# Expert weights in transfers of 4 MB with rows of 32 KB, and a feed-forward on rows that are scaled afterwards

## The chip, the cores and the metric

One Trainium2 chip (trn2), one of its cores. The metric is the device time of the whole program in microseconds (us); the kernel before ran three times, with a median of 1717.28 us (1716.75 to 1719.55).

## What is computed

Two transformer blocks, one behind the other, batch 1, width D = 1024, all in f32. The first has 272 rows (16 meta tokens and 256 of input): a norm, differential attention beside a gated convolution, and a feed-forward of 16 experts, each of which takes its 34 best rows:

```python
logits = hs @ w_router; aff = softmax(logits); g, idx = top_k(aff.T, 34)
xg = hs[idx]
y = einsum('ecf,efd->ecd', silu(xg @ w_gate) * (xg @ w_up), w_down) * g[..., None]
out = zeros((L, D)).at[idx.reshape(-1)].add(y.reshape(-1, D))
```

w_gate and w_up are 1024 x 2048 for each expert, w_down 2048 x 1024: 8 MB each, 24 MB for an expert, 384 MB (402.7 million bytes) for all. The second block works on 256 rows. Of it only the end matters here:

```python
x = x + merged @ w_out[l]
h2 = rms_norm_2(x, norm2_g[l])          # x * rsqrt(mean(x*x) + 1e-6) * g
x = x + jnp.square(jax.nn.relu(h2 @ w_ff1[l])) @ w_ff2[l]
```

w_ff1 is 1024 x 4096, w_ff2 4096 x 1024. Since relu(s a)^2 = s^2 relu(a)^2 for a positive s, the scale of a row can be left out of h2 and the row of the result multiplied by 1 / (mean(x*x) + 1e-6).

## The kernel before

The five engines each run a list of instructions written out by hand (`pe_program`, `act_program`, `dve_program`, `pool_program`, `sp_program`). They meet at named events: `mark("pe_moe", "used", slot)` counts a semaphore up, `at("used", slot)` is the value to wait for. TensorE's results stand in eight PSUM banks of 128 x 512 f32; `room(bank, ...)` waits until what the bank held before has been taken out.

**Expert weights.** A ring of 20 slots in SBUF, each of 128 partitions x 2048 f32 (1 MB, 8 KB in a partition), holds the weights. An expert has 24 slots: 16 for gate and up (k = 0 to 7, two matrices), 8 for down. They are numbered from 16 on (`expert_slot`, L430), so expert 0 has 16 to 39 and expert 15 has 376 to 399; `ring_slot` (L425) gives the place. SyncE fetches two slots with one DMA (`fetch_pair`, L2718), 2 MB in rows of 16 KB, except at two places (`HALVED`, L51) where it fetches single slots. Before it issues, it waits until TensorE has used the slots that stood there, 20 slots earlier (`freed`, L2685). All its DMAs run in one queue: the first block's weights, the experts', then those of the second block, 160 raw pieces of 512 KB (`fetch_raw`, L2742), into three buffers that lie where ring slots were. `brought(i)` (L435) names the fetch with which slot i came; TensorE waits for it in `gate_up` (L674) and `down` (L717).

**Order in an expert.** TensorE multiplies gate and up (L690), two column groups side by side, then for even experts scatters the pair of experts before (L707), turns the hidden rows (L714) and multiplies down (L728). ScalarE makes the SiLU (L1319) and copies Y (L1333, L1334), VectorE multiplies (L2010). In the first expert TensorE also gathers the rows between the k-steps (L670). In the last expert ScalarE rounds the first three raw pieces of the second block (`hi`, L1307) before it copies Y.

**Second block.** Every weight piece of 128 x 1024 is split into a rounded part (`hi`, ScalarE, L1307) and a remainder (`lo`, VectorE, L1991), in four buffers; products are made from three passes over parts. `quad` (L1113) multiplies one piece into four banks, 4 + 2 ti + db (ti: half of the rows, db: half of the columns), for the output projection (`h2o`) and for the second product of the feed-forward (`ff2`).

**Between h2o and the feed-forward.** VectorE adds the four banks into H (L2471). ScalarE squares each (L1654), VectorE makes the mean (L2477), POOL the power -1/2 (L2662), VectorE and ScalarE scale one half of the rows each into `XB2` (L2480, L1657). TensorE turns them (`turn_two`, L753), VectorE multiplies by the gain (L2036), ScalarE rounds (L1345), VectorE and POOL make the remainders (L2041, L2565). TensorE waits for all of these (`normed`, L756) before the first of 32 tiles of the feed-forward (`tile_sides`, L780; matmuls L787, L788, L790). The bank of each tile, and of each turned group in `turn_two`, is drawn from one cycle of six banks, `rot` (L744), that runs through the whole second block. Behind each tile ScalarE copies half of it (L1673), VectorE adds (L2494) and squares (L2496), ScalarE rounds (L1662), VectorE makes the remainder (L2488), in eight buffers `RL`. After `ff2` VectorE adds the four banks into H (L2506) and ScalarE stores them (L1682).

Of the kernel before, what the change touches and what calls it, by code (L numbers as in the profile page):

```python
# [191 lines left out]
class Memory:  # L192


    def __init__(self, nc):
# [55 lines left out]
        self.ring_pair = [sb(f"ring{s}", ring0 + 4096 * s, 4096) for s in range(RING // 2)]  # L251
        self.ring = [self.ring_pair[s // 2][:, 2048 * (s % 2):2048 * (s % 2) + 2048] for s in range(RING)]
# [143 lines left out]
        self.XB2 = late[:, 0:2048].rearrange("p (t c) -> p t c", t=2)  # L396
        self.tmp2 = [late[:, 2048:3072], late[:, 6144:7168]]
# [56 lines left out]
def pe_program(pe, m, sig, banks):  # L454
# [677 lines left out]
    turn_two(m.XB2, "h2")  # L1132
    normed("h2")
# [9 lines left out]
def act_program(act, m, sig, banks, t):  # L1143
# [520 lines left out]
    for i in range(32):  # L1664
# [14 lines left out]
    for ti in range(2):  # L1679
        for db in range(2):  # L1680
# [29 lines left out]
def dve_program(dve, m, sig, banks, t):  # L1710
# [755 lines left out]
    for ti in range(2):  # L2466
        for db in range(2):
# [4 lines left out]
    for ti in range(2):  # L2472
        x, y = m.fr[:, 8 + 2 * ti:9 + 2 * ti], m.fr[:, 9 + 2 * ti:10 + 2 * ti]
        dve.wait_ge(*at("s2", ti, 1))
        e.tensor_scalar(x, x, y, None, ALU.add).then_inc(*mark("dve_norm2", "s2 sum", ti))
        dve.wait_ge(*now("dve_norm2"))
        e.tensor_scalar(x, x, 1.0 / D, EPS, ALU.mult, ALU.add).then_inc(*mark("dve_norm2", "mean h2", ti))  # L2477
        dve.wait_ge(*at("power h2", ti))
        if ti == 0:
            e.tensor_scalar(m.XB2[:, 0, :], H[:, 0, :], x, None, ALU.mult).then_inc(*mark("dve_norm2", "h2", 0))  # L2480
        else:
            e.tensor_copy(m.fr[:, 10:11], x).then_inc(*mark("dve_norm2", "h2 scale", 1))
    turned("h2", m.vec[:, V_N2:V_N2 + 8], m.tmp2)
# [6 lines left out]
    for i in range(32):  # L2490
# [11 lines left out]
    for ti in range(2):  # L2502
        for db in range(2):
# [407 lines left out]
```

## Time and profile before

| | us |
|---|---|
| median of three runs | 1717.28 |
| the profiled execution | 1717.86 |
| its span | 1716.1 |
| TensorE matmuls busy | 1481.4 (86%) |
| VectorE busy | 564.4 (33%) |
| ScalarE busy | 413.9 (24%) |
| POOL busy | 107.6 (6%) |
| DMA, 511.5 MB, mean | 298 GB/s |

The span runs from the first to the last instruction of the profiled execution; its own time is 1.8 us longer. All times in the rows count from the start of the span. A busy TensorE is not TensorE at its peak: matmuls overlap, and half of the clock doubles them. A row of a stretch gives busy time and count for each engine, the granted clock of TensorE (1.00 is 2.4 GHz, 0.50 is 1.2 GHz), the share in which the 16 DMA engines were busy, and the rate.

### The profile page before, as it was taken

Reading aid. Unit: us, or ns where it says so; the run is one execution under the profiler, and the core shown is the slowest. Engines: PE = TensorE matmul, PEld = TensorE weight load, DVE = VectorE, ACT = ScalarE, POOL = GpSimd, SP = SyncE. Lnnn points to the kernel's source line nnn. Section 1 sums busy time; section 2 is a strip of 40 time slices with the busy share of each in tenths; the row PEclk is TensorE's granted clock in tenths of the full one; section 3 lists DMA queues with packets and bytes.
Section 4 is the critical chain, followed back from the end, with each engine's and each line's share of the span. In section 5 each row is a group of like instructions: output and inputs, shape, how many; then the busy total and the mean of one; then the engine's idle time right before and its main releaser. Section 6 shows DMA issues by size and latency. Waiting matters only on the chain.

```text
span 1716.1 us, 18717 instructions
## 1 busy us (share of the span) xinstructions
PE 1481.4 (86%) x7789; PEld 880.6 (51%) x7789; DVE 564.4 (33%) x966; ACT 413.9 (24%) x850; POOL 107.6 (6%) x117
## 2 busy tenths in 40 slices
PE   7999799977877878778778778699998999989999
PEld 7684433322222222222222222287897899968887
DVE  6573300100101001001001010385874555858843
ACT  5342010000000000000000000246642564445532
POOL 2010000000000000000000000021420210500000
PEclk9999799999999999999999999989999999989999
DMA  9235799999999999999999999744331334535564
GB/s 383 114 105 239 293 427 427 427 427 427 427 427 427 426 427 427 427 427 427 427 426 427 427 427 427 291 135 131 134 111 36 126 116 152 181 123 185 184 201 142
DMA packets 55989, 511.50 MB, mean 298 GB/s; under 512 B 6481, under 2 KB 6737, under 8 KB 28897
## 3 DMA queue, kind: packets, MB, share of 16 engines
q1 hardware_dynamic: 54144, 506.11, 73.3%
q10 hardware_dynamic: 1760, 4.19, 0.7%
q8 instruction: 62, 1.02, 0.2%
q14 instruction: 23, 0.18, 0.0%
HBM read 509.23 MB, written 1.05 MB: 297 GB/s over the span
## 4 chain that ended last, share of the span: by engine, by line
PE 56%; DMA 35%; DVE 4%; ACT 3%; issue 1%; POOL 0%; ACTq 0%; DVEq 0%; SPq 0%; POOLq 0%
DMA sb_ring<-in_w_gate_up 33%; PE PS L771 10%; PE PS L690 7%; PE PS L728 7%; PE PS L1118 6%; PE PS L807 4%; PE PS L788 4%; DMA sb_raw<-in_w 2%; PE PS L880 2%; PE PS L600 2%; PE PS L707 2%; PE PS L787 2%; PE PS L490 1%; PE PS L493 1%; PE PS L498 1%
## 5 line engine op out<-in xcount | busy, mean ns | idle before, releaser
L690 PE MATMUL PS<-sb_ring,sb_XG 128*64 128x512 f32 x2048 | 466.4, 601 | 120.3 <-DMA sb_ring<-in_w_gate_up 120.0
L690 PEld LDWEIGHTS PS<-sb_ring,sb_XG 128*64 128x64 f32 x2048 | 142.7, 137 | 438.4 <-issue 228.8
L2010 DVE TENSOR_TENSOR sb_SL<-sb_SL,PS 128x512 f32<-128x512 f32 x32 | 20.5, 683 | 792.4 <-PE PS L690 792.4
L728 PE MATMUL PS<-sb_ring,sb_HT 128*64 128x512 f32 x1024 | 226.1, 595 | 28.6 <-DMA sb_ring<-in_w_down 14.1
L1991 DVE TENSOR_TENSOR sb_wp<-sb_raw,sb_wp 128x1024 fp32r<-128x1024 f32 x160 | 206.7, 1294 | 115.2 <-ACT sb_wp L1307 113.9
L1307 ACT CAST sb_wp<-sb_raw 128x1024 fp32r<-128x1024 f32 x160 | 166.9, 1045 | 124.4 <-PE PS L1118 56.3
L771 PE MATMUL PS<-sb_hr,sb_wp 128*128 128x256 f32 x1440 | 183.7, 289 | 6.2 <-DVE sb_hr L2041 3.5
L771 PEld LDWEIGHTS PS<-sb_hr,sb_wp 128*128 128x128 f32 x1440 | 178.5, 196 | 10.0 <-issue 6.5
L728 PEld LDWEIGHTS PS<-sb_ring,sb_HT 128*64 128x64 f32 x1024 | 82.0, 137 | 162.4 <-issue 116.3
L1319 ACT ACTIVATE sb_SL<-PS 128x512 f32<-128x512 f32 x32 | 17.4, 595 | 516.8 <-PE PS L690 516.8
L788 PE MATMUL PS<-sb_hr,sb_wp 128*128 128x512 f32 x256 | 90.0, 405 | 3.4 <-DVE sb_hr L2041 3.4
L807 PE MATMUL PS<-sb_wp,sb_hr 128*128 128x512 f32 x336 | 83.8, 404 | 4.4 <-ACT sb_SUV L1384 4.2
L1118 PE MATMUL PS<-sb_wp,sb_fh 128*128 128x512 f32 x384 | 87.2, 389 | 0.0
L1118 PEld LDWEIGHTS PS<-sb_wp,sb_fh 128*128 128x128 f32 x384 | 72.1, 188 | 14.9
L807 PEld LDWEIGHTS PS<-sb_wp,sb_hr 128*128 128x128 f32 x336 | 63.4, 193 | 18.7 <-issue 6.1
L1333 ACT COPY sb_Y<-PS 64x512 f32<-64x512 f32 x16 | 9.2, 578 | 237.8 <-PE PS L728 237.8
L787 PE MATMUL PS<-sb_hr,sb_wp 128*128 128x256 f32 x224 | 63.4, 283 | 0.0
L2554 POOL TENSOR_TENSOR sb_sm<-sb_sm 128x1 f32<-128x1 f32 x2 | 1.1, 548 | 945.7 <-DVE sb_sm L2051 945.7
L788 PEld LDWEIGHTS PS<-sb_hr,sb_wp 128*128 128x128 f32 x256 | 47.0, 193 | 12.7 <-issue 3.7
L787 PEld LDWEIGHTS PS<-sb_hr,sb_wp 128*128 128x128 f32 x224 | 43.3, 193 | 1.6
L707 PE MATMUL PS<-sb_Y,sb_GT 128*128 128x512 f32 x64 | 31.3, 634 | 4.0 <-ACT sb_Y L1334 4.0
L2654 POOL TENSOR_TENSOR sb_NN<-sb_NN,sb_SC 128x256 f32<-128x256 f32 x24 | 25.4, 1059 | 96.2 <-DVE sb_SC L2454 93.4
(396 smaller groups left out, 1357.8 us busy)
## 6 DMA issues: line engine op xcount, KB each, us to landing
sb_ring<-in_w_gate_up SPq DMA_DIRECT2D x127, 2048.0 KB, 45.2
sb_ring<-in_w_down SPq DMA_DIRECT2D x63, 2048.0 KB, 45.2
sb_raw<-in_w SPq DMA_DIRECT2D x160, 512.0 KB, 4.0
sb_ring<-in_w_in SPq DMA_DIRECT2D x12, 1024.0 KB, 15.9
sb_ring<-in_w_out SPq DMA_DIRECT2D x4, 1024.0 KB, 13.9
sb_ring<-in_w_gate_up SPq DMA_DIRECT2D x2, 1024.0 KB, 9.7
sb_ring<-in_w_down SPq DMA_DIRECT2D x2, 1024.0 KB, 45.0
sb_KW<-in_kw SPq DMA_DIRECT2D x1, 1403.0 KB, 34.7
```

Source lines behind the costliest of these rows:

```text
L600: ins = e.matmul(PS[0:n, b, :], m.mixT[:, c, c0:c0 + n], w[:, o:o + 512], start=(c == 0), stop=(c == 7))
L690: ins = e.matmul(PS[64 * g:64 * g + 64, b, :], m.XG[:, k, r0:r0 + 64], m.ring[s][:, (2 * g + q) * 512:(2 * g + q) * 512 + 512], start=(k = ...
L707: e.matmul(PS[:, b, :], m.GT[:, ti, :], m.Y[:, db * 512:db * 512 + 512], start=True, stop=True).then_inc(*mark("pe_moe", "in", "sc", p, ti ...
L728: ins = e.matmul(PS[64 * g:64 * g + 64, b, :], m.HT[:, c % 8, (c // 8) * 64:(c // 8) * 64 + 64], m.ring[s][:, a * 1024 + g * 512:a * 1024 ...
L771: ins = e.matmul(PS[:, b, 0:256], lhs(p1, k), rhs(p2, k), start=(k == 0 and q == 0), stop=(k == K - 1 and q == 2))
L787: e.matmul(PS[:, b, 0:256], lo[:, k, :], m.hT[0][:, k, :], start=False, stop=False)
L788: ins = e.matmul(PS[:, b, :], hi[:, k, :], m.hT2[:, k, :, :], start=(k == 0), stop=(k == 7))
L807: ins = e.matmul(PS[:, b, :], m.hT[p1][:, k, ti * 128:ti * 128 + 128], w[p2][:, k2 * 512:k2 * 512 + 512], start=(k == 0 and q == 0), stop= ...
L880: ins = e.matmul(PS[:, b, r * 128:r * 128 + 128], lhs(4 * q + r), rhs(4 * q + r), start=True, stop=True)
L1118: ins = e.matmul(PS[:, b, :], acts[p1][:, k, ti * 128:ti * 128 + 128], w[p2][:, db * 512:db * 512 + 512], start=(k == 0 and q == 0), stop= ...
L1307: e.copy(m.wp_hi[n % WR], m.raw[raw_turn(n) % RAW]).then_inc(*mark("act_split", "hi", n))
L1991: e.tensor_tensor(m.wp_lo[n % WR], m.raw[raw_turn(n) % RAW], m.wp_hi[n % WR].bitcast(F32), ALU.subtract).then_inc(*mark("dve_split", "lo", n))
```

## The change

Three things are changed for the experts' weights. The array in HBM is laid out so that four slots lie in one row of 32 KB. SyncE fetches slots 44 to 395 four at a time, 4 MB in one DMA, and waits until all four places are free; slots 16 to 43 and 396 to 399 are fetched as before. TensorE waits for the fetch that brought its slot.

In the second block the scale of h2 is left out. TensorE turns H itself, for 256 columns of both row halves into one bank, and needs for that only the column half whose adds are done; `quad` and the adds go through the column halves first. ScalarE makes the rounded part from PSUM with the gain as scale, 128 x 256 for each k, VectorE the remainder in the same way. TensorE waits for them k by k. The sums of squares are made by ScalarE behind tiles 4 and 6, mean and reciprocal by VectorE behind tiles 8 and 10, and the last adds multiply by it. POOL has no part in this norm any more, and `XB2` and its temporaries are gone.

```diff
+PAIRS = tuple(range(16, 24 + RING, 4)) + (16 + 24 * 16 - 4,)
...
-        self.ring_pair = [sb(f"ring{s}", ring0 + 4096 * s, 4096) for s in range(RING // 2)]
-        self.ring = [self.ring_pair[s // 2][:, 2048 * (s % 2):2048 * (s % 2) + 2048] for s in range(RING)]
+        self.ring_four = [sb(f"ring{s}", ring0 + 8192 * s, 8192) for s in range(RING // 4)]
+        self.ring = [self.ring_four[s // 4][:, 2048 * (s % 4):2048 * (s % 4) + 2048] for s in range(RING)]
...
 def brought(i):
+    if i - i % 4 not in PAIRS:
+        return i - i % 4
     return i if i - i % 2 in HALVED else i - i % 2
...
     def tile_sides(n, *tile):
         hi, lo = (x.rearrange("p (k c) -> p k c", k=8) for x in piece(n))
         b = room(next(rot), *tile)
         for k in range(8):
+            pe.wait_ge(*at("h2 hi", k))
+            pe.wait_ge(*(at("out", "h2", k // 2) if k % 2 else at("h2 lo", k)))
...
     def quad(k, last, acts, w, name):
-        for ti in range(2):
-            for db in range(2):
+        for db in range(2):
+            for ti in range(2):
...
-    turn_two(m.XB2, "h2")
-    normed("h2")
+    for j in range(4):
+        b = room(j, "h2", j)
+        for k2 in range(2):
+            for ti in range(2):
+                pe.wait_ge(*at("out", "h2o", ti, j // 2))
+                c = 256 * j + 128 * k2
+                ins = e.transpose(PS[:, b, 256 * k2 + 128 * ti:256 * k2 + 128 * ti + 128], m.H[:, ti, c:c + 128], ident)
+        ins.then_inc(*mark("pe_norm", "in", "h2", j))
...
-    act.wait_ge(*at("in", "h2o", 1, 1))
-    for ti in range(2):
-        for db in range(2):
-            act.wait_ge(*at("out", "h2o", ti, db))
-            e.activation(m.RL[:, 2 * ti + db, :, :].rearrange("p q c -> p (q c)"), H[:, ti, db * 512:db * 512 + 512], ACT.Square,
-                         accum_out=m.fr[:, 8 + 2 * ti + db:9 + 2 * ti + db]).then_inc(*mark("act_norm2", "s2", ti, db))
-    act.wait_ge(*at("h2 scale", 1))
-    e.activation(m.XB2[:, 1, :], H[:, 1, :], ACT.Copy, scale=m.fr[:, 10:11]).then_inc(*mark("act_norm2", "h2", 1))
-    turned("h2", m.tmp2)
+    for k in range(8):
+        act.wait_ge(*at("in", "h2", k // 2))
+        act.wait_ge(*at("in", "h2o", 1, 1))
+        e.mul(m.hT[0][:, k, :], PS[:, banks.of("h2", k // 2), 256 * (k % 2):256 * (k % 2) + 256],
+              m.vec[:, V_N2 + k:V_N2 + k + 1]).then_inc(*mark("act_norm2", "h2 hi", k))
+
+    def row_sums(ti):
+        act.wait_ge(*now("act_sums"))
+        e.activation(m.JKf, H[:, ti, :], ACT.Square, accum_out=m.fr[:, 8 + ti:9 + ti]).then_inc(*mark("act_sums", "sums", "h2", ti))
...
+        if i in (4, 6):
+            row_sums(i // 2 - 2)
...
+    for k in range(8):
+        j = k // 2
+        event = ("out", "h2", j) if k % 2 else ("h2 lo", k)
+        dve.wait_ge(*at("h2 hi", 2 * j + 1))
+        e.scalar_tensor_tensor(m.hT[1][:, k, :], PS[:, banks.of("h2", j), 256 * (k % 2):256 * (k % 2) + 256], m.vec[:, V_N2 + k:V_N2 + k + 1],
+                               m.hT[0][:, k, :].bitcast(F32), ALU.mult, ALU.subtract).then_inc(*mark("dve_norm2", *event))
...
+        if i in (8, 10):
+            r = m.fr[:, 4 + i // 2:5 + i // 2]
+            dve.wait_ge(*at("sums", "h2", i // 2 - 4))
+            e.tensor_scalar(r, r, 1.0 / D, EPS, ALU.mult, ALU.add).then_inc(*mark("dve_norm2", "mean h2", i // 2 - 4))
+            dve.wait_ge(*now("dve_norm2"))
+            e.reciprocal(r, r).then_inc(*mark("dve_norm2", "h2 scale", i // 2 - 4))
...
-            e.tensor_tensor(hv, hv, PS[:, banks.of("ff2", ti, db), :], ALU.add).then_inc(*mark("dve_ff", "out", "ff2", ti, db))
+            dve.wait_ge(*at("h2 scale", ti))
+            e.scalar_tensor_tensor(hv, PS[:, banks.of("ff2", ti, db), :], m.fr[:, 8 + ti:9 + ti], hv, ALU.mult, ALU.add).then_inc(*mark("dve_ff", "out", "ff2", ti, db))
...
-    def fetch_pair(i, src):
+    def fetch_four(i, src):
+        for j in range(4):
+            if brought(i + j) == i + j:
+                n = sum(brought(i + q) == i + j for q in range(4))
+                s, o = ring_slot(i + j), 2048 * j
+                for q in range(n):
+                    for event in freed(i + j + q):
+                        sp.wait_ge(*at(*event))
+                e.dma_start(m.ring_four[s // 4][:, o:o + 2048 * n], src[:, o:o + 2048 * n]).then_inc(*mark(f"ring{s}", "w", i + j, by=16))
```

## Rows read from the trace of the kernel before

**Rows 1.** The page: the span, and the DMA rates of 40 slices.
```profile
span 1716.1 us, 18717 instructions
...
GB/s 383 114 105 239 293 427 427 427 427 427 427 427 427 426 427 427 427 427 427 427 426 427 427 427 427 291 135 131 134 111 36 126 116 152 181 123 185 184 201 142
```

**Rows 2.** The chain in order of time (start us, length us, what), end of the experts.
```profile
1063.17 35.68 DMA sb_raw<-in_w
1098.87 1.05 ACT sb_wp L1307
```

**Rows 3.** Stretches: busy time of each engine, TensorE's clock, DMA share, GB/s.
```profile
34.00:44.00 10.00, 10.00 (x77) 9.77 (x76) 6.12 (x9) 5.11 (x8) 3.30 (x3) 1.00 1.01 419
...
616.00:675.00 59.00, 44.99 (x196) 14.56 (x196) 5.30 (x10) 2.83 (x5) 0.00 (x0) 1.00 1.01 427
```

**Rows 4.** The page: DMA issues, count, KB each, median us from issue to landing.
```profile
sb_ring<-in_w_gate_up SPq DMA_DIRECT2D x127, 2048.0 KB, 45.2
```

**Rows 5.** Pair fetches (L2727): issued 126-200, at 193.0, 202-213, at 217.0; later issues.
```profile
DMA to landing us min/median/max: 7.7/10.9/18.5
...
DMA to landing us min/median/max: 9.0/9.0/9.0
...
L2727 SPq DMA_DIRECT2D sb_ring<-in_w_gate_up x3: 328/328/328, 202.6 to 212.2; - x3
...
DMA to landing us min/median/max: 10.1/10.2/10.3
...
DMA to landing us min/median/max: 10.4/10.4/10.4
...
225.17 0.33 SPq L2727 DMA_DIRECT2D sb_ring<-in_w_gate_up  x1
L2727 SPq DMA_DIRECT2D sb_ring<-in_w_down x3: 328/328/328, 242.9 to 249.8; - x3
```

**Rows 6.** Timeline of the last expert: start, length, engine, line, operation, idle before.
```profile
1075.55 3.65 PE L690 MATMUL PS<-sb_ring,sb_XG 128*64 128x512 f32 x16 [2.00 <-DMA sb_ring<-in_w_gate_up]
1082.30 7.09 PE L728 MATMUL PS<-sb_ring,sb_HT 128*64 128x512 f32 x32 [0.98 <-DVE sb_HT L2024]
1090.12 7.09 PE L728 MATMUL PS<-sb_ring,sb_HT 128*64 128x512 f32 x32 [0.73 <-DMA sb_ring<-in_w_down]
```

**Rows 7.** Timeline from the output projection to the feed-forward, and its second product.
```profile
1518.63 2.65 PE L1118 MATMUL PS<-sb_wp,sb_hr 128*128 128x512 f32 x11
1520.88 2.47 DVE L2471 TENSOR_TENSOR sb_H<-sb_H,PS 128x512 f32<-128x512 f32 x4
1532.88 0.77 PE L788 MATMUL PS<-sb_hr,sb_wp 128*128 128x512 f32 x1 [3.38 <-DVE sb_hr L2041]
...
1538.37 0.37 ACT L1673 COPY sb_late<-PS 128x256 f32<-128x256 f32 x1 [6.55 <-PE PS L788]
...
1625.10 7.21 PE L1118 MATMUL PS<-sb_wp,sb_fh 128*128 128x512 f32 x31
```

**Rows 8.** TensorE's clock around that norm and at the kernel's start.
```profile
1525.00:1526.00 1.00, 0.85 (x4) 0.85 (x5) 0.37 (x3) 0.00 (x0) 0.52 (x1) 0.50 0.00 0
...
8.64 4.51 PE L474 MATMUL PS<-sb_cst,sb_XN 128*128 128x128 f32 x24 [8.64 <-DVE sb_sm L1722]
...
16.00:18.00 2.00, 2.00 (x11) 2.00 (x12) 2.00 (x6) 2.00 (x3) 0.00 (x0) 0.58 1.01 418
18.00:20.00 2.00, 2.00 (x11) 2.00 (x11) 2.00 (x4) 0.40 (x1) 0.00 (x0) 0.57 1.02 422
```

**Rows 9.** Groups by line (count, busy us, mean ns), and the feed-forward's stretch.
```profile
L2461 DVE SCALAR_TENSOR_TENSOR sb_hr<-sb_NN,sb_hr 128x256 fp32r<-128x256 f32 x8 | 3.7, 531 | 0.0
L2454 DVE SCALAR_TENSOR_TENSOR sb_SC<-sb_R,PS 128x256 f32<-128x256 f32 x14 | 5.6, 412 | 2.0 <-POOL sb_NN L2654 2.0
L1645 ACT ACTIVATE sb_hr<-sb_NN 128x256 fp32r<-128x256 f32 x8 | 2.6, 403 | 1.8 <-PE PS L771 1.8
...
1535.00:1625.00 90.00, 90.00 (x507) 78.34 (x506) 73.96 (x123) 50.12 (x92) 0.00 (x0) 0.98 0.55 180
```

More of the change, by code:

```diff
@@ L1678, in act_program @@
         hi(P_FF2 + i + 3)
-    for ti in range(2):
-        for db in range(2):
+    for db in range(2):
+        for ti in range(2):
             act.wait_ge(*at("out", "ff2", ti, db))
@@ L2463, in dve_program @@
         lo(P_OUT + c + 3)
-    for ti in range(2):
-        for db in range(2):
+    for db in range(2):
+        for ti in range(2):
             hv = H[:, ti, db * 512:db * 512 + 512]
@@ L2471, in dve_program @@
             e.tensor_tensor(hv, hv, PS[:, banks.of("h2o", ti, db), :], ALU.add).then_inc(*mark("dve_merge", "out", "h2o", ti, db))
[L2472 to L2483, printed above, removed]
+    for k in range(8):
[4 more added lines that the diff above has]
+                               m.hT[0][:, k, :].bitcast(F32), ALU.mult, ALU.subtract).then_inc(*mark("dve_norm2", *event))
     def hidden_lo(i):
@@ L2501, in dve_program @@
         lo(P_FF2 + i + 3)
-    for ti in range(2):
-        for db in range(2):
+    for db in range(2):
+        for ti in range(2):
             hv = H[:, ti, db * 512:db * 512 + 512]
             dve.wait_ge(*at("in", "ff2", ti, db))
-            e.tensor_tensor(hv, hv, PS[:, banks.of("ff2", ti, db), :], ALU.add).then_inc(*mark("dve_ff", "out", "ff2", ti, db))
+            dve.wait_ge(*at("h2 scale", ti))
+            e.scalar_tensor_tensor(hv, PS[:, banks.of("ff2", ti, db), :], m.fr[:, 8 + ti:9 + ti], hv, ALU.mult, ALU.add).then_inc(*mark("dve_ff", "out", "ff2", ti, db))
 def pool_program(pool, m, sig, banks, t):
@@ L2655, in pool_program @@
             n += 1
-    for ti in range(2):
-        x = m.fr[:, 8 + 2 * ti:9 + 2 * ti]
-        pool.wait_ge(*at("mean h2", ti))
-        pool.wait_ge(*now("pool_norm"))
-        e.tensor_tensor(x, x, mhalf[:, 0:1], ALU.pow).then_inc(*mark("pool_norm", "power h2", ti))
-    first_half_lo("h2", m.tmp2)
 def sp_program(sp, m, sig, banks, t):
@@ L2716, in fetch @@
         e.dma_start(m.ring[s], src).then_inc(*mark(f"ring{s}", "w", i, by=16))
-    def fetch_pair(i, src):
-        if i in HALVED:
-            fetch(i, src[:, 0:2048])
-            fetch(i + 1, src[:, 2048:4096])
-        else:
-            s = ring_slot(i)
-            for event in freed(i) + freed(i + 1):
-                sp.wait_ge(*at(*event))
-            e.dma_start(m.ring_pair[s // 2], src).then_inc(*mark(f"ring{s}", "w", i, by=16))
+    def fetch_four(i, src):
[7 more added lines that the diff above has]
+                e.dma_start(m.ring_four[s // 4][:, o:o + 2048 * n], src[:, o:o + 2048 * n]).then_inc(*mark(f"ring{s}", "w", i + j, by=16))
     for i in range(12):
@@ L2733, in sp_program @@
     for ex in range(NE):
-        for k in range(8):
-            fetch_pair(expert_slot(ex, 2 * k), t["w_gate_up"][ex, k])
-        for s in range(4):
-            fetch_pair(expert_slot(ex, 16 + 2 * s), t["w_down"][ex, s])
+        for k in range(4):
+            fetch_four(expert_slot(ex, 4 * k), t["w_gate_up"][ex, k])
+        for s in range(2):
+            fetch_four(expert_slot(ex, 16 + 4 * s), t["w_down"][ex, s])
     done = {}
@@ L2845, in layout @@
     a["w_out"] = pack_R(i["w_out"][0])
-    a["w_gate_up"] = np.concatenate([i[n][0].reshape(NE, 8, 128, 2048) for n in ("w_gate", "w_up")], 3)
-    a["w_down"] = np.ascontiguousarray(i["w_down"][0].reshape(NE, 4, 4, 128, D).transpose(0, 1, 3, 2, 4)).reshape(NE, 4, 128, 4 * D)
+    g = np.stack([i[n][0].reshape(NE, 4, 2, 128, 2048) for n in ("w_gate", "w_up")], 3)
+    a["w_gate_up"] = np.ascontiguousarray(g.transpose(0, 1, 4, 2, 3, 5)).reshape(NE, 4, 128, 8192)
+    a["w_down"] = np.ascontiguousarray(i["w_down"][0].reshape(NE, 2, 8, 128, D).transpose(0, 1, 3, 2, 4)).reshape(NE, 2, 128, 8 * D)
     v = np.zeros((P, NVEC), np.float32)
```

9 lines of the change are left out of this document (2 added, 7 removed).

## The prediction, made before the changed kernel was run

> **What bounds the kernel now.** I read the page first, then the chain of waits, stretches of the timeline and the DMA queue of SyncE. The page [rows 1] gives 1716.1 us of span and a strip of DMA rates in which twenty of forty slices stand at 426 or 427 GB/s: in the middle something is limited by transfers. The chain in order of time [rows 2] shows how that stretch ends: behind the expert weights stand the first raw weights of the second block (35.68 us from issue to landing), then ScalarE's rounding of them, then its copy of the last expert's output. So between about 200 us and 1100 us the DMA stream sets the time, and what shortens it moves all that comes after. From 1100 us on TensorE is the bound, with one hole that this change touches, the norm between the second block's output projection and its feed-forward.
>
> The stream's own pace: with rows of 16 KB it moves 427 GB/s, with rows of 8 KB (the first block's weights) 419 GB/s [rows 3], each with a DMA share of 1. Per engine, a sixteenth, a 16 KB row takes 16384 B / 26.69 = 613.9 ns and an 8 KB row 8192 B / 26.19 = 312.8 ns. Two short rows take 11.7 ns more than one long row: a cost per row. The neighbouring windows read 420 GB/s in places, which makes 10.3 ns of it; I take 10.9.
>
> **Part 1: longer rows.** Before, the experts come in transfers of 2 MB, 127 of them for gate and up alone [rows 4]. Slots 16 to 43 and 396 to 399 stay as they were; the 352 slots between them go from 176 pairs to 88 fours. Each engine then moves 8 rows of 32 KB where it moved 16 of 16 KB: 88 x 8 = 704 rows fewer on each engine. At 10.9 ns that is **-7.7 us** (-7.3 to -8.2). No transfer in this trace has rows above 16 KB, so the outer ends are 0 (the cost goes with bytes above some length) and a loss (a rival below). I take the straight line because 8 and 16 KB lie next to 32.
>
> The trace's row costs 10.9 ns. The Trainium skill ("DMA: Bandwidth & Descriptors", the section on why small descriptors are slow) states a fixed overhead of about 3 cycles per packet; with the 850 MHz of the same page that is an estimate of 3.5 ns, so 704 rows would bring 2.5 us and not 7.7. Measured rows say more than the page, and I go by them; the page's value is a rival below.
>
> **Part 2: what a coarser grain costs where the ring is nearly dry.** SyncE may issue a transfer only when TensorE has used all its slots. In the first expert it is just in time: a pair is issued every 4.8 us while one takes 4.9 us to move. Three issues from 202.6 to 212.2 us show that, the second of them (slots 42 and 43) landing at 207.4 + 10.2 = 217.6 us. The issue at 217.0 us (slots 46 and 47, after slot 27 is used) lands 10.4 us later, at 227.4 us; the one at 193.0 us, into an empty queue, needs 9.0 us, and the quickest 2 MB up to 200 us needs 7.7 us [rows 5]. Since 4.9 us of these are movement, the start of a transfer takes 2.8 to 4.1 us. Slots 44 to 47, so far two issues (212 and 217 us), become one, at 217.0. It finds a queue that is about to end, at 217.6 us, and lands at 217.0 + 2.8 to 4.1 + 9.7 = 229.5 to 230.8 us instead of 227.4: 2.1 to 3.4 us of the stream are lost and never come back. I take **+2.8**. The next fours are issued when slots 31, 35 and 39 are used. The pairs that waited for the first and the last of these were issued at 225.2 and 242.9 us [rows 5], slot 35 is used 7.1 us before slot 39 [rows 6], at 235.8, against queue ends near 230, 240 and 249.5: leads of 4 us and more, so no second hole, and the lead grows from there. In the median 45.2 us pass from issue to landing [rows 4], so later about four fours are always queued, and TensorE's 7.1 us for a four instead of 3.65 for a pair [rows 6] take nothing from the stream. In SyncE's queue only the raw weights stand behind the experts', and they are asked for 35 us before they land [rows 2].
>
> **Part 3: the end of the experts.** The last two k-steps of gate and up (slots 388 to 391) now arrive together, when the last pair of them did, so TensorE ends gate and up 3.4 us later against the stream. Before, it took up the last pair at 1075.55 for 3.65 us, began the down projection at 1082.30 (3.1 us of SiLU and turning between), had caught up with the stream at 1090.12 and finished at 1097.2; ScalarE was busy with the raw weights until 1099.92 and only then copied [rows 6]. Laid out again with fours: 7.1 us of gate and up from 1075.5, the same 3.1 us, and 14.1 us for the eight slots of down, which are then all there, end at 1099.8. That is 0.1 us before ScalarE: the cover is all but gone. The four is 9.7 us on its way and 7.1 in work; TensorE's pauses of some 2.6 us between could cost it the clock once; half speed for the 3.4 us that such a fall lasts in [rows 8] is 1.7 us. I charge **+0.3** (0 to +1.7).
>
> **Part 4: the feed-forward on unscaled rows.** Before, TensorE ends the output projection at 1521.3; the adds into H run to 1523.35; then squares, POOL's power, scaling, 16 transposes, gains, rounding and remainders, and the first matmul of the feed-forward starts at 1532.88, 11.6 us after the last [rows 7]. The change takes POOL, the squares, the scaling and four 128x512 temporaries out of this path. New path, from rows: VectorE begins its adds at 1520.9 (it makes the remainder of the third piece first), so the first two adds end at 1522.2, the four at 1523.4. Four transposes per bank, 0.19 us each at the kernel's start [rows 8], put bank 0 there at about 1523.1. ScalarE: eight products of 128x256 at 0.40 us (the nearest rounding row) from 1523.1, two before VectorE begins at 1523.95. VectorE: eight remainders at 531 ns (the same operation and output type; 412 ns is that of one that reads PSUM and writes plain f32) end at 1523.95 + 4.25 = 1528.2 [rows 9]. The first tile of the feed-forward looks as if it could follow k by k, but its bank is the one of the fourth h2 bank (the turning list of six banks stands at 3 there, since the norm no longer draws four from it), which is released by the last remainder. So it starts at 1528.3: **-4.6 us** (-5.6 with 412 ns).
>
> The granted clock is the second term. From 1525 us on it is at half [rows 8], 3.7 us into TensorE's idleness, and the first tile takes 5.5 us (1532.88 to 1538.37) instead of the 2.8 us of the others (31 tiles to 1625.1 [rows 7]): 2.7 us. After the change TensorE rests 0.9 us, transposes for 3 us, rests 3.1 us. The nearest case in the trace is the kernel's start: 24 transposes from 8.64 to 13.15 at a full clock, a rest of 2.75 us, and a mean clock of 0.58 and 0.57 in the 4 us from 16, which makes 3.4 us at half [rows 8]. So I take one such fall behind the rest: 1.7 of the 2.7 us still lost, **-1.0 us** (0 to -2.7). The Trainium skill ("TensorE: Matmul & The Clock Gate", PE-mode transpose) says that transposes do not count as busy for the gate; by it the rest would be 7 us in one and all 2.7 us would stay lost. The rows at the kernel's start speak against it, weakly.
>
> What moves elsewhere: the row sums go to ScalarE beside tiles 4 and 6 (two of about 1.25 us, where it is busy 50 of 90 us), their mean and reciprocal to VectorE beside tiles 8 and 10 (four of about 0.2 us, where it is busy 74 of 90 us [rows 9]). A tile leaves VectorE 0.3 us spare and there are eight buffers and four pieces of lead, so I cost them at nothing; without that cover it would be 0.8 us. The four last adds become fused ones: 412 against 421 ns in the two forms at 128x256, so 0. The new order of quadrants keeps the matmuls and 0.
>
> **Sum.** -7.7 + 2.8 + 0.3 - 4.6 - 1.0 = -10.2 us. The profiled execution took 1717.86 us for a span of 1716.1, and becomes 1707.7; the median of three before is 1717.28, 0.6 lower, so 1707.1. With all bounds one way it is -14 (1703), the other way -6.4 (1711).
>
> **Rivals.** *Length buys nothing*: the engines cut or pace rows so that 32 KB cost twice 16 KB. For it: no row of that length is here. Then -2.5, 1714.8 us. *The page's 3.5 ns*: -5.0, 1712.3 us. *The feed-forward gives nothing net*: the start comes earlier, but the clock stays low longer or VectorE, late with pieces, holds the next tiles; against it, VectorE's spare time. Then -4.6, 1712.7 us. *Slower, by the pace of long rows*: the sixteen engines read places twice as far apart, and the stream falls to the slowest saturated pace that a row shows, 419 GB/s. The 88 fours are 369.1 MB: 880.9 us instead of 864.4, +16.5 in place of -7.7, so 1731.3 us. It decides from a pace of 425.8 GB/s down, where the loss eats the 2.5 us of the rest; that the pace rises from 8 to 16 KB speaks against it.
>
> **How the numbers follow.** Forecast 0.66; nothing from length 0.10; the page's value 0.10; no feed-forward gain 0.09; slower pace 0.05. 0.2% (3.4 us) is about what a measurement of this kernel can tell from no change. The forecast, the page's value and the third rival lie below 1713.9: 0.85 faster. The first rival is the 0.09 within the bound; the slower pace, and a little of the first, is 0.06. The range goes from 1702.5 to 1714.0, over the forecast's own 1703 to 1711 to the two rivals at 1712.
>
> **What would show it.** Right: 431 GB/s in the middle; an expert each 58.3 us instead of 58.9; a hole of 2 to 3 us in the stream near 218 us; ScalarE's copy of the last Y about 5 us earlier; no more than 7.5 us between the last matmul of the output projection and the first of the feed-forward. Wrong: 427 GB/s or less, holes in the stream at later experts, the last Y copy waiting for TensorE, or a first tile of 5.5 us.

## The result, and the profile after

The kernel after takes **1704.78 us** (median of four runs, 1703.32 to 1705.47); the kernel before, run beside it, 1718.41. The ratio is 0.992, with a 95% interval of 0.9903 to 0.9937: faster, by 0.6% to 1.0%. The profiled execution took 1705.39 us, 12.5 us less than the one of before, and its span is shorter by the same 12.5 us. The page, first the span and the rates, then the DMA issues:

```profile
span 1703.6 us, 18612 instructions
...
GB/s 383 117 100 222 305 406 430 430 432 433 430 430 430 429 430 433 430 430 430 430 430 433 431 433 430 321 123 144 121 103 58 122 112 151 176 157 186 185 196 138
...
sb_ring<-in_w_gate_up SPq DMA_DIRECT2D x59, 4096.0 KB, 39.9
sb_ring<-in_w_down SPq DMA_DIRECT2D x29, 4096.0 KB, 41.3
```

Beside [rows 1]: slices of 427 have become 429 to 433, and one, the sixth, has fallen from 427 to 406. That one (213 to 256 us) holds the hole in the stream. The 88 fours are there (59 and 29), and about four of them are under way at a time (39.9 us at 9.7 each). The packets that the page counts in SyncE's queue fall from 54144 to 41472. The difference is 16 times 792, so 792 on each of the 16 engines: the 704 rows of the prediction and 88 more, one for each transfer that is saved. A row of 32 KB is not cut in two.

The same stretches as [rows 3] and around 217 us, kernel after:

```profile
330.00:1050.00 720.00, 587.29 (x2522) 199.79 (x2518) 43.61 (x78) 35.14 (x62) 0.00 (x0) 0.96 1.00 431
214.50:216.00 1.50, 1.50 (x10) 0.44 (x7) 0.00 (x0) 0.00 (x0) 0.00 (x0) 1.00 0.79 339
216.00:217.50 1.50, 1.50 (x10) 0.69 (x7) 0.00 (x0) 0.00 (x0) 0.00 (x0) 1.00 0.03 11
217.50:219.00 1.50, 1.50 (x10) 0.85 (x10) 0.44 (x1) 1.22 (x2) 0.00 (x0) 1.00 1.31 350
```

And kernel before:

```profile
330.00:1050.00 720.00, 571.52 (x2518) 188.36 (x2514) 43.61 (x78) 35.12 (x62) 0.00 (x0) 1.00 1.01 427
...
216.00:217.50 1.50, 1.50 (x11) 0.71 (x6) 0.00 (x0) 0.00 (x0) 0.00 (x0) 1.00 0.89 382
```

The last column is the rate: 431 against 427 GB/s in the long stretch, 11 against 382 in the 1.5 us of the hole. The column before last but one, TensorE's clock, says something that the prediction did not have: 0.96 instead of 1.00 over 720 us, so about 58 us of them at half clock. Its busy time grows by 16 us for the same work and costs nothing, as TensorE waits for weights there anyway.

The fetch of slots 44 to 47, kernel after (issue, and time to landing), which stands against the last two landings of [rows 5]:

```profile
L2730 SPq DMA_DIRECT2D sb_ring<-in_w_gate_up x1: 328/328/328, 217.1 to 217.1; - x1
...
DMA to landing us min/median/max: 13.5/13.5/13.5
```

The end of the experts and the scatter, kernel after, timeline of TensorE and ScalarE:

```profile
1060.19 7.09 PE L692 MATMUL PS<-sb_ring,sb_XG 128*64 128x512 f32 x32 [2.64 <-DMA sb_ring<-in_w_gate_up]
1069.90 8.64 PE L692 MATMUL PS<-sb_ring,sb_XG 128*64 128x512 f32 x32 [2.63 <-DMA sb_ring<-in_w_gate_up]
...
1081.65 13.95 PE L730 MATMUL PS<-sb_ring,sb_HT 128*64 128x512 f32 x64 [0.99 <-DVE sb_HT L2033]
...
1094.85 1.05 ACT L1318 CAST sb_wp<-sb_raw 128x1024 fp32r<-128x1024 f32 x1 [0.22 <-DMA sb_raw<-in_w]
1095.92 0.58 ACT L1344 COPY sb_Y<-PS 64x512 f32<-64x512 f32 x1
...
1097.15 3.70 PE L709 MATMUL PS<-sb_Y,sb_GT 128*128 128x512 f32 x8 [1.55 <-ACT sb_Y L1345]
```

The scatter of the kernel before:

```profile
1101.18 5.40 PE L707 MATMUL PS<-sb_Y,sb_GT 128*128 128x512 f32 x8 [3.97 <-ACT sb_Y L1334]
```

ScalarE's third rounding begins at 1094.85 instead of 1098.87 [rows 2]: the experts end 4.0 us earlier. TensorE is done at 1081.65 + 13.95 = 1095.60, ScalarE at 1095.90: the cover, 2.7 us before, has shrunk to 0.3 us. The scatter takes 1.7 us less, as the clock does not fall in it.

From the output projection to the feed-forward, kernel after:

```profile
1515.47 2.47 DVE L2480 TENSOR_TENSOR sb_H<-sb_H,PS 128x512 f32<-128x512 f32 x4
1516.20 0.14 PEld L1143 LDWEIGHTS PS<-sb_cst,sb_H 128*128 128x128 f32 x1 [0.76 <-DVE sb_H L2480]
...
1516.80 2.18 PE L1143 MATMUL PS<-sb_cst,sb_H 128*128 128x128 f32 x15 [0.27 <-DVE sb_H L2480]
1517.39 3.03 ACT L1664 ACTIVATE sb_hr<-PS,sb_vec 128x256 fp32r<-128x256 f32 x8 [3.09 <-PE PS L1143]
...
1518.26 3.23 DVE L2485 SCALAR_TENSOR_TENSOR sb_hr<-PS,sb_vec,sb_hr 128x256 fp32r<-128x256 f32 x8 [0.32 <-ACT sb_hr L1664]
...
1521.75 0.47 PE L793 MATMUL PS<-sb_hr,sb_wp 128*128 128x512 f32 x1 [2.76 <-DVE sb_hr L2485]
...
1524.80 0.37 ACT L1680 COPY sb_late<-PS 128x256 f32<-128x256 f32 x1 [3.45 <-PE PS L793]
...
1612.46 0.70 PE L1123 MATMUL PS<-sb_wp,sb_fh 128*128 128x512 f32 x2 [1.01 <-DVE sb_late L2497]
```

The last matmul of the output projection ends at 1515.87, so 5.9 us lie between it and the first tile, where 11.6 were. The first tile waits until the last of eight remainders (L2485) has run, and takes 3.05 us (1521.75 to 1524.80) where it took 5.49 [rows 7]. The last line is new: TensorE waits 1.0 us before `ff2`, for VectorE's add behind the last tile (L2497).

| from before to after, profiled executions | before | after | difference |
|---|---|---|---|
| start of the last scatter | 1101.18 | 1097.15 | -4.0 |
| scatter until the projections of the second block | 20.11 | 18.44 | -1.7 |
| projections until the end of the output projection | 399.99 | 400.28 | +0.3 |
| from there to the first tile | 11.60 | 5.88 | -5.7 |
| first tile until `ff2` | 92.22 | 90.71 | -1.5 |
| `ff2` until the end | 91.0 | 91.1 | +0.1 |
| span | 1716.1 | 1703.6 | -12.5 |

### The profile page after: what moved, and what is told of

It reads as the page before. It is cut to its first block, busy times and chain, and to the rows that moved or that the text cites. A ratio compares the mean times of both kernels' runs of the same rounds, so it can differ in the third digit from the quotient of the medians.

```text
span 1703.6 us, 18612 instructions
## 1 busy us (share of the span) xinstructions
PE 1490.3 (87%) x7789; PEld 888.2 (52%) x7789; DVE 560.7 (33%) x966; ACT 413.2 (24%) x849; POOL 103.6 (6%) x113
## 4 chain that ended last, share of the span: by engine, by line
PE 57%; DMA 34%; DVE 4%; ACT 3%; issue 1%; POOL 0%; ACTq 0%; SPq 0%; DVEq 0%; POOLq 0%
DMA sb_ring<-in_w_gate_up 29%; PE PS L773 10%; PE PS L692 9%; PE PS L730 6%; PE PS L1123 6%; PE PS L812 4%; PE PS L793 4%; DMA sb_raw<-in_w 3%; DMA sb_ring<-in_w_down 2%; PE PS L885 2%; PE PS L602 2%; PE PS L792 2%; PE PS L709 2%; PE PS L492 1%; PE PS L500 1%
## 5 line engine op out<-in xcount | busy, mean ns | idle before, releaser
L692 PE MATMUL PS<-sb_ring,sb_XG 128*64 128x512 f32 x2048 | 479.6, 623 | 110.1 <-DMA sb_ring<-in_w_gate_up 110.1
L692 PEld LDWEIGHTS PS<-sb_ring,sb_XG 128*64 128x64 f32 x2048 | 152.0, 143 | 431.8 <-issue 274.8
L812 PE MATMUL PS<-sb_wp,sb_hr 128*128 128x512 f32 x336 | 84.0, 404 | 4.4 <-ACT sb_SUV L1395 4.3
L812 PEld LDWEIGHTS PS<-sb_wp,sb_hr 128*128 128x128 f32 x336 | 63.4, 193 | 18.6 <-issue 6.1
L793 PEld LDWEIGHTS PS<-sb_hr,sb_wp 128*128 128x128 f32 x256 | 45.8, 188 | 11.6 <-ACT sb_wp L1318 3.0
L492 PE MATMUL PS<-sb_hnhi,sb_wh 128*128 128x272 f32 x160 | 27.8, 320 | 4.7 <-ACT sb_hnhi L1189 3.3
## 6 DMA issues: line engine op xcount, KB each, us to landing
sb_ring<-in_w_gate_up SPq DMA_DIRECT2D x59, 4096.0 KB, 39.9
sb_ring<-in_w_down SPq DMA_DIRECT2D x5, 2048.0 KB, 13.6
```

Source lines behind the costliest of these rows:

```text
L492: e.matmul(PS[:, b, 0:L], hi[:, k, :], m.hnp[0][:, k, :], start=(k == 0), stop=False)
L692: ins = e.matmul(PS[64 * g:64 * g + 64, b, :], m.XG[:, k, r0:r0 + 64], m.ring[s][:, (2 * g + q) * 512:(2 * g + q) * 512 + 512], start=(k = ...
L812: ins = e.matmul(PS[:, b, :], m.hT[p1][:, k, ti * 128:ti * 128 + 128], w[p2][:, k2 * 512:k2 * 512 + 512], start=(k == 0 and q == 0), stop= ...
```

## The experiments

Ten kernels. The kernel before took 1717.22 us beside `experts_only`, `feedforward_only`, `pairs_to_56` and `banks_shifted`, 1717.07 beside `rows16_in_4mb`, `grain_alone`, `all_mended` and `rows32_in_2mb`, and 1717.72 beside `rows16_half_partitions` and `rows32_every_second`. Beside the kernel after it took 1718.41, 1.2 to 1.3 us more than beside the first eight, so part of a difference between medians of different series is this shift; each ratio goes by its own series. My theory was the sum of the prediction; the rivals were that the number or size of the transfers brings the gain and not the length of the rows, that the feed-forward gives nothing net, and, for what is still lost, that the hole, the last four and the wait on bank 3 are not its causes.

**One half at a time.** `experts_only` has the diff's hunks on `PAIRS`, `ring_four`, `brought`, `fetch_four` and the layout in HBM, `feedforward_only` all the others.

> The expert part of the change alone, the feed-forward as before. My theory by the traces of before and after: ScalarE's third rounding of raw weights, which ended at 1099.92 us before, ends 4.0 us earlier, and the scatter behind it runs at the full clock (3.7 us instead of 5.4), so the sum is -5.7 us against the kernel before, the stretch from 1121 us on as long as before. The rival, that nearly all of the gain is the feed-forward's and the 4 MB transfers only change the noise, wants -1 us or less here.

> The feed-forward part alone, transfers as before. My theory: the first matmul of the feed-forward 5.7 us earlier against the end of the output projection, 2.4 us because its first tile runs at the full clock, and 1.0 us lost at the start of the second product, where bank 4 is held by the last tile: together -7.1 us against the kernel before. If the clock falls in the shorter rest all the same, -5. If the two parts add up, this and the experts alone come to the -12.5 us of the whole change's span.

The experts alone: 1709.51 us (1708.38 to 1710.63), ratio 0.9955 (0.9942 to 0.9969), -7.7 us. The feed-forward alone: 1712.14 (1710.12 to 1713.06), 0.9972 (0.9961 to 0.9984), -5.1 us. Both halves are faster by themselves, and -7.7 and -5.1 together are -12.8, where the whole has -12.5 in the profiled executions and -13.6 in the medians: neither lives on the other. Each is some 2 us from what I expected, in opposite directions. The traces say where most of it lies. The start of the last scatter moves by -3.6 us with the experts alone (-4.0 in the kernel after), and the rest before the first tile by -5.7 us with the feed-forward alone, as in the kernel after. But a long stretch of block 2 that no edit touches, from the first product behind its twelve tiles of queries, keys and values (L807 before, L812 after) to the start of its output projection, took 339.8 us in the one and 343.7 in the other, against 341.4 before. So a sum of parts is good to about 2 us and no better.

**Length, number or grain.** Two kernels keep the waits of the kernel after, but the layout in HBM is that of before, with rows of 16 KB.

`rows16_in_4mb` has 88 transfers of 4 MB, and each row of the ring is filled from two rows of 16 KB:

```diff
-                e.dma_start(m.ring_four[s // 4][:, o:o + 2048 * n], src[:, o:o + 2048 * n]).then_inc(*mark(f"ring{s}", "w", i + j, by=16))
+                if n == 4:
+                    e.dma_start(m.ring_four[s // 4].rearrange("p (k c) -> p k c", k=2), src.rearrange("k p c -> p k c")).then_inc(*mark(f"ring{s}", "w", i + j, by=16))
...
```

`grain_alone` has 176 pairs of 2 MB, but SyncE waits for four free slots and then issues two pairs, and TensorE waits for both:

```diff
+    def arrived(slot):
+        pe.wait_ge(*at("w", brought(slot)))
+        if slot - slot % 4 not in PAIRS:
+            pe.wait_ge(*at("w", brought(slot) + 2))
...
+                for q in range(0, n, 2) if n == 4 else (0,):
...
```

> The changed kernel, with 4 MB in one transfer as before the run, but HBM laid out as in the kernel before, so that a transfer moves rows of 16 KB, two for each partition. If the cost hangs on the row (my theory), the stream between 330 and 1050 us stands at 427 GB/s and the third rounding of raw weights ends about 7 us later than in the changed kernel (1095.9 us), near 1103 us. If it hangs on the number of transfers, 431 GB/s and 1096 us.

> The changed kernel with transfers of 2 MB in rows of 16 KB as before the change, but both waits in fours: SyncE issues two pairs when four places are free, TensorE starts when four slots are there. It has the cost of the grain without the gain of the rows. My theory: a hole of about 3 us in the stream at 216 us, 427 GB/s after it, TensorE's clock falling in the pauses as in the changed kernel (about 20 falls against 1 before), the third rounding at 1103 us, 3 us after that of the kernel before. If long transfers and not the grain make the hole, there is none and 1100 us.

`rows16_in_4mb`: 1713.45 us (1711.74 to 1714.21, ten runs), ratio 0.9977 (0.9968 to 0.9987). `grain_alone`: 1715.13 (1712.87 to 1718.74, ten runs), 0.999 (0.9981 to 1.0). The interval of the second reaches 1.0, so it can't be told from the kernel before. The long stretch of both, `rows16_in_4mb` first, and for `grain_alone` the 3 us of the hole too:

```profile
330.00:1050.00 720.00, 582.72 (x2505) 197.32 (x2502) 43.61 (x78) 35.15 (x62) 0.00 (x0) 0.96 1.01 427
```

```profile
330.00:1050.00 720.00, 582.21 (x2512) 221.31 (x2510) 43.69 (x78) 35.14 (x62) 0.00 (x0) 0.96 1.01 427
216.00:219.00 3.00, 3.00 (x18) 1.50 (x16) 0.44 (x1) 1.39 (x2) 0.00 (x0) 1.00 0.46 98
```

Both stay at 427 GB/s, the pace of before: it is the rows of 32 KB that bring the 431, and not the transfers of 4 MB. The kernel after differs from `rows16_in_4mb` by the rows alone, and its median is 8.7 us lower. Of that, the traces give the rows 6.5 us: ScalarE's third rounding ends at 1095.90 against 1102.40. The profiled executions are 6.3 us apart, since a fall of the clock in the first tile of `rows16_in_4mb` (1.6 us more) and a shorter way from the projections to the output projection (1.7 us less) nearly cancel. Against the kernel before, with its third rounding at 1099.92, `rows16_in_4mb` is 2.5 us late and `grain_alone` (1103.14) 3.2: that is the hole, and the 0.7 us between them may be the 88 packets that the first saves on each engine. Of the 5.1 us that the feed-forward gives alone, 3.6 are left in `rows16_in_4mb` and 1.9 in `grain_alone`. In `grain_alone` the Y copy waits 2.6 us for TensorE (it ends at 1105.73, ScalarE at 1103.14), as the last four comes late there. And a clock of 0.95 or 0.96 in the long stretch comes with all kernels of this grain that keep the stream, whatever their rows.

**The hole alone.** Slots 16 to 55 in pairs instead of 16 to 43.

```diff
-PAIRS = tuple(range(16, 24 + RING, 4)) + (16 + 24 * 16 - 4,)
+PAIRS = tuple(range(16, 56, 4)) + (16 + 24 * 16 - 4,)
```

> The changed kernel with pairs up to slot 55 and fours from slot 56 on. My theory: the hole in the DMA stream at 216 us goes (3.2 us), three fours less save 0.26 us less, so the third rounding of raw weights ends 3 us earlier, -3 us against the changed kernel. Rival: the stream makes the hole good later, since TensorE has spare time in the experts, and the end stays where it is.

1706.68 us (1703.02 to 1707.48), ratio 0.9933 (0.992 to 0.9945): not faster than the kernel after, so my -3 us was wrong. The hole is gone, and ScalarE's third rounding ends at 1093.20 instead of 1095.90. Then two things take the gain. Stretch, TensorE and ScalarE of this kernel:

```profile
216.00:219.00 3.00, 3.00 (x18) 1.68 (x18) 0.44 (x1) 1.67 (x2) 0.00 (x0) 1.00 0.97 415
```

```profile
1078.65 15.65 PE L730 MATMUL PS<-sb_ring,sb_HT 128*64 128x512 f32 x64 [0.99 <-DMA sb_ring<-in_w_down]
```

```profile
1094.34 0.58 ACT L1344 COPY sb_Y<-PS 64x512 f32<-64x512 f32 x1 [1.14 <-PE PS L730]
```

The down projection takes 15.65 us instead of 13.95, one fall of the clock, and ends at 1094.30, 1.1 us after ScalarE. So TensorE, which the prediction had ready 0.1 us ahead of ScalarE, is now the later one: of 2.7 us, 1.6 reach the scatter. The rest went in the stretch that no edit touches. First the kernel after, then this one:

```profile
1152.53:1493.86 341.33, 323.97 (x2226) 289.65 (x2225) 213.14 (x353) 172.67 (x416) 75.12 (x72) 0.98 0.37 123
```

```profile
1151.18:1495.89 344.71, 328.02 (x2227) 292.74 (x2225) 212.92 (x353) 172.68 (x416) 75.12 (x72) 0.97 0.36 122
```

The same matmuls take 3.4 us longer at a lower mean clock (0.97 against 0.98), with VectorE and ScalarE busy for the same time. Over the ten traces that keep the stream, the stretch goes from 339.8 us (a clock of 0.99, `experts_only` and `grain_alone`) to these 344.7 (0.97), so the time follows the clock; why a run gets more or fewer falls is open.

**The bank.** The prediction said that the first tile could follow the norm k by k but for its bank. Two draws from the cycle of banks ahead of the tiles give it another:

```diff
+    next(rot), next(rot)
     for i in range(32):
         tile_sides(P_FF1 + i, "ff1", i).then_inc(*mark("pe_ff", "in", "ff1", i))
```

> The changed kernel with two more draws from the cycle of six banks, so that the first tile of the feed-forward has a bank that is free at once and the last tile is not in bank 4. My theory: the 1.0 us pause before the second product goes, and the first tile follows the remainders k by k instead of waiting for the last of them, so that it ends about 2.3 us earlier: -3 us against the changed kernel, 1701.5 us. If the pause of VectorE's remainders is what counts and not the bank, -1 us or nothing.

1700.82 us (1699.58 to 1704.3), ratio 0.9909 (0.9895 to 0.9922). The median is 4.0 us below that of the kernel after, 2.8 us if each is set against its own runs of the kernel before, and the intervals of the two ratios overlap; the trace decides:

```profile
1514.80 2.18 PE L1143 MATMUL PS<-sb_cst,sb_H 128*128 128x128 f32 x15 [0.27 <-DVE sb_H L2481]
1516.89 0.47 PE L793 MATMUL PS<-sb_hr,sb_wp 128*128 128x512 f32 x1
...
1606.76 0.62 PE L1123 MATMUL PS<-sb_wp,sb_fh 128*128 128x512 f32 x2
```

```profile
1516.26 3.23 DVE L2486 SCALAR_TENSOR_TENSOR sb_hr<-PS,sb_vec,sb_hr 128x256 fp32r<-128x256 f32 x8 [0.32 <-ACT sb_hr L1665]
```

The first tile starts at 1516.89, while VectorE still makes remainders, 3.0 us after the output projection instead of 5.9. `ff2` starts with no idle time in its row, so the new 1.0 us pause was the same cycle of banks: with six banks and 32 tiles, the four draws that the norm no longer makes had moved the last tile from bank 2 to bank 4, which `ff2` needs first, and two more draws move it to bank 0. From the output projection to `ff2` the two make 96.6 - 92.9 = 3.7 us.

**All together.** Pairs up to slot 55, pairs for slots 388 to 395, and the shifted banks.

> The changed kernel with pairs up to slot 55, the fours from 388 and 392 as pairs again, and the six banks shifted by two. My theory: ScalarE's third rounding at 1093.3 us (no hole) and TensorE done with the last expert before it, so that the scatter starts 1.3 us after that; the first tile of the feed-forward starts 3 us after the output projection instead of 5.9 and the second product without a pause: -2.5 and -4 us, 1698 us, give or take the 2 us by which the stretch between 1155 and 1490 us differs from run to run. Rival: TensorE rests longer before the scatter and its clock falls there as before the change: 1.7 us of it come back.

**1699.44 us** (1697.46 to 1702.57), ratio 0.9896 (0.9881 to 0.9911), the lowest of all: its median is 5.3 us below that of the kernel after, 4.0 us if each is set against its own runs of the kernel before. Stretch, TensorE and ScalarE:

```profile
216.00:219.00 3.00, 3.00 (x18) 1.54 (x16) 0.44 (x1) 1.08 (x2) 0.00 (x0) 1.00 0.99 426
```

```profile
1084.77 7.07 PE L730 MATMUL PS<-sb_ring,sb_HT 128*64 128x512 f32 x32
1095.06 3.70 PE L709 MATMUL PS<-sb_Y,sb_GT 128*128 128x512 f32 x8 [3.23 <-ACT sb_Y L1346]
```

No hole (426 GB/s), and with pairs at the end TensorE is done at 1091.84, 2.0 us ahead of ScalarE: the scatter starts at 1095.06, 2.1 us before that of the kernel after. It takes 3.70 us behind a rest of 3.23, so the rival's fall of the clock did not come. Its interval overlaps that of `banks_shifted` (1.4 us apart), so only the trace shows what the pairs add. A last comparison of this kind, pairs at the end alone, was not run.

**Half of the partitions.** I wanted long rows in small transfers, and cut each four into its partitions 0 to 63 and 64 to 127:

```diff
+                if n == 4:
+                    for h in range(2):
+                        r = slice(64 * h, 64 * h + 64)
+                        event = ("w", i + j) if h else ("w half", i + j)
+                        e.dma_start(m.ring_four[s // 4][r, :], src[r, :]).then_inc(*mark(f"ring{s}", *event, by=16))
...
```

> The changed kernel, with rows of 32 KB but each four as two transfers of 2 MB over 64 partitions each. If the cost hangs on the row: 431 GB/s and the third rounding ends at 1096 us, as in the changed kernel. If on the number of transfers: 427 GB/s and 1103 us.

2613.89 us (2602.16 to 2624.29), ratio 1.5217: neither theory had that. Two more kernels took the causes apart, the one with the same halves and rows of 16 KB, the other with `slice(h, 128, 2)`, every second partition, and rows of 32 KB.

> The expert weights of slots 44 to 395 in transfers of 1 MB over 64 partitions each, in rows of 16 KB (the rows of the kernel before), with the waits of the fours. The stream fell to 210 GB/s when each 4 MB were cut into two transfers of 64 partitions with rows of 32 KB. If the half number of partitions does that (one such transfer at a time keeps only half of the paths into SBUF at work), this kernel falls to the same 210 GB/s and about 2610 us. If it is the rows of 32 KB that need all 128 partitions, this one stays at 427 GB/s and about 1715 us.

> As the kernel after, but each 4 MB cut into two transfers of 64 partitions: the even ones, then the odd ones, rows of 32 KB. If what halves the stream is that one half of SBUF (64 partitions side by side) is written at a time, the even and odd partitions lie over all of it and the stream comes back to 431 GB/s, about 1705 us. If it is the number of rows in a transfer (64 over 16 engines), it stays at 210 GB/s, about 2610 us.

2582.24 us and 1706.90 us (one run each). The long stretch of `rows32_in_2mb`, `rows16_half_partitions` and `rows32_every_second`, in this order:

```profile
330.00:1050.00 720.00, 349.85 (x1232) 108.46 (x1230) 21.81 (x39) 16.99 (x30) 0.00 (x0) 0.73 1.01 210
```

```profile
330.00:1050.00 720.00, 350.01 (x1232) 117.65 (x1230) 21.84 (x39) 18.15 (x32) 0.00 (x0) 0.73 1.01 212
```

```profile
330.00:1050.00 720.00, 592.94 (x2522) 200.31 (x2518) 43.62 (x78) 35.14 (x62) 0.00 (x0) 0.95 1.00 430
```

Not the rows (16 and 32 KB alike at half speed), and not the size of the transfer or its 64 rows (those of every second partition run at 430 GB/s), but which 64 rows it takes: 64 side by side halve the stream. The edit changes two things at once, the partitions that are written and the places in HBM that are read (one piece of 2 MB, or every second row of 4 MB). The read is the unlikely cause, since the kernel before reads its weights in pieces of 2 MB as well, at 427 GB/s; no run separates the two. The DMA engines show a busy share of 1.01 all the while, so that column does not tell the two cases apart; the rate does. The Trainium skill ("SBUF — State Buffer", Door 1: The DMA port swizzle) says that a transfer's bandwidth depends on how many of the 16 ports its partitions reach, and that partitions 64 apart lie on the two different ports of a cluster: partitions 0 to 63 reach eight. The even ones of all 128 would by its mapping reach sixteen. The traces agree with that rule: 210 and 430 GB/s. As a test of row length with small transfers, `rows32_every_second` does what `rows32_in_2mb` was meant for: rows of 32 KB in transfers of 2 MB keep 430 GB/s.

## Why the prediction was right

Foretold 1707.1 us in a range of 1702.5 to 1714.0, measured 1704.78; -10.2 us on the profiled execution's time, measured -12.5. The mechanisms of the four parts were right; two sizes were off (a remainder of VectorE, the clock in the first tile), and two effects were in no term. By its steps:

- **Part 1, the rows, -7.7.** Right. The stream runs at 431 GB/s. The experts end 4.0 us earlier with a hole of 3.2, which makes 7.2 us for the rows and the 88 saved transfers, 9.1 ns for each of the 792 packets; against `rows16_in_4mb` the rows alone bring 6.5 us, 9.2 ns for each of 704. The straight line through 8 and 16 KB, at 10.9 ns, held to 32 KB within 16%. The rival with 3.5 ns a row would give 2.5 us: it is out, and so are "length buys nothing" (427 GB/s) and the slower pace.
- **Part 2, the hole, +2.8.** Right in place and size. The four was issued at 217.1 and landed at 230.6 (foretold 229.5 to 230.8), 3.2 us after the landing of before; `rows16_in_4mb` and `grain_alone` put the hole at 2.5 and 3.2 us. The later issues, at 225.3, 236.2 and 243.1, land 13.9 to 16.7 us on, and no second hole appeared. That a refill with finer grain removes it is shown by the 415 and 426 GB/s of the two kernels with pairs up to slot 55.
- **Part 3, the end, +0.3.** Came out at 0 in this trace, by luck: two errors cancel. The clock did fall once in the last k-steps (8.64 us instead of 7.09, the bound of +1.7 in the prediction), but the last four arrived 1.6 us earlier against the raw weights than I had laid it out: 24.95 us lie between its first matmul and the third rounding, 23.3 before. I have no cause for the second. The tie itself is real: in `experts_only`, `grain_alone`, `pairs_to_56` and `banks_shifted` the copy of Y waits for TensorE (0.2, 2.6, 1.1 and 0.3 us), which the prediction had named as a sign of being wrong.
- **Part 4, the start of the feed-forward, -4.6.** Measured -5.7, the value that the prediction had as its bound with 412 ns (-5.6). The mechanism was right (the first tile waits for the bank of the last remainder: with another bank, in `banks_shifted`, it starts before that remainder), one duration was wrong. I took 531 ns for a remainder, the mean of the eight of L2461 [rows 9]. That mean mixes two kinds: two of the eight, at 829 and 952 ns, ran while POOL was at work, the other six took 410 to 413. The new remainders take 477 ns, and as each starts 0.39 us after the one before, eight take 3.23 us instead of 4.25. So neither the type that is written nor the place that is read made the 531: six remainders that read SBUF and write fp32r took what the operations of L2454, which read PSUM, did (412). Why the new ones take 477 was not tested. L2461 and POOL before, then the remainders after:

```profile
L2461 DVE SCALAR_TENSOR_TENSOR sb_hr<-sb_NN,sb_hr x2: 829/890/952, 1498.3 to 1499.0; 128x256 fp32r<-128x256 f32 x2
L2461 DVE SCALAR_TENSOR_TENSOR sb_hr<-sb_NN,sb_hr x6: 410/410/413, 1499.9 to 1501.6; 128x256 fp32r<-128x256 f32 x6
...
1498.12 1.60 POOL L2654 TENSOR_TENSOR sb_NN<-sb_NN,sb_SC 128x256 f32<-128x256 f32 x2 [1.49 <-DVE sb_SC L2454]
```

```profile
L2485 DVE SCALAR_TENSOR_TENSOR sb_hr<-PS,sb_vec,sb_hr x8: 477/477/486, 1518.3 to 1521.0; 128x256 fp32r<-128x256 f32 x8
```

- **The clock, -1.0.** Measured -2.4 for the first tile: no fall at all. With the same rest of 5.9 us the clock stayed at full in `feedforward_only`, `pairs_to_56` and `rows32_every_second` as well, and fell in `rows16_in_4mb`, inside the first tile, and in `grain_alone`, before it (0.67 from 1528.0 to 1529.2 us, 0.50 from 1529.3 on, when the tile starts); `ff2` came 1.6 and 2.7 us later there than in the kernel after. So the fall that I charged can be had, in two cases of six, and in one of them it costs the whole 2.7 us. The Trainium skill ("TensorE: Matmul & The Clock Gate", Part 4: PE-mode transpose) says that transposes do not count as busy for the clock gate. Before the change the clock was at half 3.7 us into TensorE's idleness; if the transposes did not count, the 5.9 us would be one such idleness, and the first tile would have started at half in all six. It did so in `grain_alone` alone: five traces speak against that statement.
- **What was missing.** *The pause before `ff2`*, +1.0: the prediction followed the shifted cycle of banks to the first tile and not to the last one. *The scatter*, -1.7: TensorE's rest ahead of it was shorter (1.55 us, 3.97 before), and the clock did not fall in it. But it took 3.70 us in the eight other kernels that keep the stream too, also in `feedforward_only`, which leaves the experts as they were and rests 3.4 us there; so it is not shown that the expert change did it. That these two nearly cancel was luck. *The falls of the clock through the experts* (0.96): off the path everywhere but in the last expert.
- **Row sums, mean, last adds, 0.** Right: the second product until the end takes 91.1 us, 91.0 before. With -5.1 us for `feedforward_only`, the rival that the feed-forward gives nothing net is out.
- **The range.** The bounds that the prediction shows add up to -6.8 us on the slow side and not to -6.4 (1710.5 us instead of 1711); the measured time lies far from that end.

The change of the profiled execution lies 2.3 us under the forecast: -1.1 from the remainders, -1.4 and -1.7 from clock falls that did not come, +1.0 from the pause, and about +0.6 in the experts and +0.3 from the projections to the end of the output projection. The medians are further apart: the kernel before took 1718.41 us beside the kernel after and 1717.28 in the three runs that the forecast started from, so their difference is -13.6, 3.4 us beyond the forecast's.

## What to carry to other kernels

When a stream of weights is the bound, price a layout by two windows at a full DMA share with different row lengths: the cost per row from 8 and 16 KB held for 32 KB within 16%. Before a group's mean duration goes into a sum, ask for its shortest, median and longest, and for what ran beside the long ones. Then look at the place where the ring is nearly dry, and keep the fine grain there and at the stream's last work; a transfer that waits for twice as many slots costs its start-up once, for good. And when an instruction list gives or takes draws from a rotating list of buffers, follow the rotation to the last user of the list and not only to the first.

## What the hardware showed that was not expected

- Transfers to 64 neighbouring partitions run at half the rate (210 to 212 GB/s) with a DMA share of 1.01, transfers over every second partition at 430.
- With fours, TensorE works 7.1 us and rests 2.6 us in gate and up, and its mean clock from 330 to 1050 us is 0.96; with pairs it works 3.65 us and rests 1.25 us, and the clock is 1.00 (0.99 in `feedforward_only`). A line of the kernel before:

```profile
1069.90 3.65 PE L690 MATMUL PS<-sb_ring,sb_XG 128*64 128x512 f32 x16 [1.26 <-DMA sb_ring<-in_w_gate_up]
```

- The same instructions in the same order take between 339.8 and 344.7 us in ten traces, longer where the mean clock is lower. An edit worth 2 us elsewhere can't be judged from one span.
- Two operations of VectorE took 829 and 952 ns beside POOL, six of the same form 410 to 413 without it.
- Of the same 5.9 us between TensorE's products, with transposes in them, four traces show no fall of the clock, one shows it within the first tile behind and one before that tile.
